# Modulation loads on ScalarE's queue, softmax statistics written in runs of four, norm roots by tile, and the output weights of the dilated layer rounded sooner

## The reference, cut to what matters

```python
for g, (window, dil) in enumerate(DIL_GROUPS):
    qkv = (h @ w_in[:, base:base + 3 * MIXER_WIDTH]).reshape(B, T, 3, DIL_HEADS, DIL_HEAD_DIM)
    o, lse = dilated_group(rope(q), rope(k), v, window, dil)
wts = jax.nn.softmax(jnp.stack(lses, axis=0), axis=0)
o = jnp.einsum('gbth,gbthd->bthd', wts, jnp.stack(outs, axis=0))
```

```python
shift, scale, gate = jnp.split((silu(c) @ w_mod + b_mod)[:, None, :], 3, axis=-1)   # w_mod: 1024 x 3072 per layer
h = rms(x, g_pre) * (1.0 + scale) + shift
```

## Time and profile before

| | |
|---|---|
| median of 3 runs | 1818.31 us (1816.36 to 1821.93) |
| the profiled execution | 1822.41 us, span 1820.6 us |
| mean granted clock of TensorE | 0.954 |
| busy: TensorE, VectorE, ScalarE, GpSimd | 93%, 52%, 35%, 11% of the span |
| DMA | 161 MB, 89 GB/s over the span |

### The profile page before, as it was taken

One profiled execution on the slowest core, in us unless ns is written; L12 is line 12 of the kernel. 1 busy time (PEld: TensorE's weight loads), 2 busy tenths in 40 slices (PEclk: granted clock), 3 DMA queues, 4 the chain that ended last, 5 costly groups with the idle time before them and its releaser, 6 DMA issues.

```text
span 1820.6 us, 22789 instructions
## 1 busy us (share of the span) xinstructions
PE 1684.1 (93%) x8922; PEld 1309.3 (72%) x8922; DVE 953.1 (52%) x1671; ACT 641.0 (35%) x1226; POOL 194.3 (11%) x221
## 2 busy tenths in 40 slices
PE   7999977989999989969999999979998999997997
PEld 6866756877788878847888878845556877785553
DVE  1233272265655555554446777446674377664462
ACT  3254342333223323343312434244442234423331
POOL 3045223100000000031001000000101010000000
PEclk9998988999999999989999999969999999997699
DMA  7211043322663673641322110230002332221000
GB/s 265 67 39 58 24 175 97 103 75 74 176 175 83 169 175 89 211 97 50 121 101 86 52 52 31 93 127 1 12 12 87 104 122 56 73 93 70 1 12 35
DMA packets 170834, 161.34 MB, mean 89 GB/s; under 512 B 39958, under 2 KB 153864, under 8 KB 170696
## 3 DMA queue, kind: packets, MB, share of 16 engines
q1 hardware_dynamic: 167592, 150.04, 27.4%
q0 software_dynamic: 2848, 9.74, 1.5%
q10 hardware_dynamic: 288, 0.10, 0.0%
HBM read 149.80 MB, written 11.18 MB: 88 GB/s over the span
## 4 chain that ended last, share of the span: by engine, by line
PE 76%; DVE 14%; ACT 4%; issue 4%; POOL 1%; DMA 1%; ACTq 0%; DVEq 0%; POOLq 0%
PE psum L2398 42%; PE psum L2369 11%; PE psum L2861 7%; PE psum L2427 6%; PE psum L2418 4%; DVE arena L1829 2%; PE psum L2532 2%; PE psum L2471 2%; PE psum L2452 1%; DVE stat L2278 1%; DVE wring_r L1906 1%; DVE arena L1808 1%; DVE psum L2227 1%; DVE wring_r L1912 1%; DVE arena L1805 1%
## 5 line engine op out<-in xcount | busy, mean ns | idle before, releaser
L2398 PE MATMUL psum<-hT_r,wring_r 128*128 128x512 f32 (+1 forms) x1768 | 595.9, 395 | 7.7 <-ACT arena L1441 3.0
L2398 PEld LDWEIGHTS psum<-hT_r,wring_r 128*128 128x128 f32 (+1 forms) x1768 | 331.8, 188 | 89.3 <-issue 13.2
L2398 PE MATMUL psum<-arena_r,wring_r 128*128 128x256 f32 (+2 forms) x1416 | 381.8, 336 | 2.6 <-DVE arena_r L1952 1.8
L1441 ACT ACTIVATE arena<-psum 128x512 f32<-128x512 f32 (+5 forms) x255 | 149.4, 611 | 475.9 <-PE psum L2398 259.6
L2398 PEld LDWEIGHTS psum<-arena_r,wring_r 128*128 128x128 f32 (+1 forms) x1416 | 228.2, 190 | 32.0 <-issue 4.2
L2369 PE MATMUL psum<-arena 128*128 128x96 f32 (+9 forms) x1460 | 238.0, 390 | 4.7 <-ACT arena L1441 2.4
L2369 PEld LDWEIGHTS psum<-arena 128*128 128x128 f32 (+5 forms) x1460 | 170.7, 203 | 68.8 <-issue 45.8
L2398 PE MATMUL psum<-arena_r 128*128 128x512 f32 (+2 forms) x680 | 210.1, 350 | 0.0
L2427 PE MATMUL psum<-ident,arena 128*128 128x128 f32 (+2 forms) x1028 | 142.1, 290 | 47.9 <-DVE arena L1808 18.4
L2427 PEld LDWEIGHTS psum<-ident,arena 128*128 128x128 f32 (+2 forms) x1028 | 122.4, 149 | 69.0 <-DVE arena L1808 20.3
L2398 PE MATMUL psum<-hT_r,arena_r 128*128 128x512 f32 (+1 forms) x408 | 163.2, 400 | 5.4 <-DVE wring_r L1906 3.7
(11 more groups left out here) (223 smaller groups left out, 1933.3 us busy)
## 6 DMA issues: line engine op xcount, KB each, us to landing
wring<-in_w_in_b SPq DMA_DIRECT2D x54, 512.0 KB, 5.9
arena<-in_w_mod SPq DMA_DIRECT2D x16, 1536.0 KB, 10.1
wring<-in_w_in SPq DMA_DIRECT2D x16, 1536.0 KB, 6.8
wring<-in_w_out SPq DMA_DIRECT2D x8, 2048.0 KB, 11.0
wring<-in_w_in_a SPq DMA_DIRECT2D x5, 1536.0 KB, 6.6
arena<-x_dram SPq DMA_DIRECT2D x3, 2048.0 KB, 11.4
wring<-in_w_in SPq DMA_DIRECT2D x6, 1024.0 KB, 5.5
arena<-ebias_dram SPq DMA_DIRECT2D x144, 32.0 KB, 1.8
```

Of the source, the lines that this page charges most:

```text
L1441: return nc.scalar.activation(out, in_, ACT.Copy, scale=scale)
L2398: ins_ = nc.tensor.matmul(b[0:hi.shape[2], 0:width], w[:, k], v[:, k], start=k + p == 0, stop=(k, p) == (KT - 1, 2))
```

## The change

- **Modulation loads.** They leave SP's list. ScalarE issues them: `mod_after` names the step after which each goes out (piece 0 after `mPV A`, 1 after `mPV B`, piece n + 1 after `mod` n), with a wait until TensorE has done that step. Piece 14 gets a buffer of its own and is loaded after `BS 4`, piece 15 after `mod` 13.
- **Modulation products.** The first moves to between `wout A` and `hT B`; one of head 4 goes; in head 5 two stand directly behind `BS 5` and none between the gates. They are 0 | 1, 2 | three in each of heads 1 to 3 | 12, 13 | 14, 15.
- **Statistics.** Group 0 is saved in two DMAs of 128 runs of four floats, in a DRAM layout of its own, and loaded back element by element in four DMAs of 32 partitions. So four saves and six loads, before three and three. In SP's order they now come directly behind `BS h`, and the bias transfers behind them.
- **Roots by tile.** GpSimd takes a tile's root ahead of its save; VectorE scales tile t - 1 after the additions of tile t; `hT B` turns the first three tiles for 7 of the 8 blocks as they come.
- **Output weights.** All four residues of each half on VectorE, in both layers; `wide B 1` moves from behind `BPV 5` to directly behind `wide B 0`, with other room.

```diff
--- before.py
+++ after.py
@@ -166,7 +166,21 @@
     add("", "outs", "wout", "A", 0, (6, 7))
+    chunk_no = itertools.count()
+
+    def modulation():
+
+        n = next(chunk_no)
+        if n:
+            l, j = divmod(n - 1, MODS)
+            add("v", "modC", l, j)
+            if j == MODS - 1:
+                add("", "modT", l)
+        if n < 2 * MODS:
+            add("v", "mod", *divmod(n, MODS))
+
     add("v" * 8, "wout", "A")
+    modulation()
     add("v" * 8, "hT", "B")
@@ -178,19 +192,6 @@
 
-    chunk_no = itertools.count()
-
-    def modulation():
...
     for h in range(BH):
@@ -201,14 +202,16 @@
             add("aav", "Bproj", h + 1, 1)
-            modulation()
+            if h + 2 < BH:
+                modulation()
             add("avav", "BT", h)
             add("aav", "Bproj", h + 1, 2)
         else:
+            modulation()
             add("", "wide", "wout", "B", 0)
+            add("", "wide", "wout", "B", 1)
             add("a", "gate", "B", 5)
             add("", "Bw", h)
-            modulation()
             add("a", "gate", "B", 6)
@@ -216,7 +219,6 @@
     add("", "outs", "wout", "B", 0, (5,))
-    add("", "wide", "wout", "B", 1)
     add("v" * 6, "wout", "B")
@@ -601,7 +603,7 @@
         xn = at(6144, TT, D)
-        mslot = at(10240, KT, MODC)
+        mslots = [at(10240, KT, MODC), at(14336, KT, MODC)]
         modpart = at(29184, MODC)
@@ -689,11 +691,11 @@
         wide_room = {("wout", "A"): [18688 + 1024 * i for i in range(8)],
-                     ("wout", "B"): [17408 + 1024 * i for i in range(6)] + [6144, 7168]}
+                     ("wout", "B"): [17408 + 1024 * i for i in range(6)] + [27136, 28160]}
 
         gate_dram = dram("gate_dram", [2, 2, D])
         x0_dram = dram("x0_dram", [T, D])
-        st0_dram = dram("st0_dram", [BH, 2, T])
+        st0_dram = dram("st0_dram", [BH, P // DIL, 2, DIL, TT])
         st12_dram = dram("st12_dram", [BH, 4, T])
@@ -876,7 +878,7 @@
             if n < split_bounds[2]:
-                return (24576, 28664, 27640)[u]
+                return (24576, 6144, 7168)[u]
             return 6144 + KT * P * u
@@ -1106,6 +1104,10 @@
 
+        mod_last = 2 * MODS - 1
+        mod_after = {("mPV", "A"): 0, ("mPV", "B"): 1, ("BS", BH - 2): mod_last - 1, mod_key(mod_last - 2): mod_last}
+        mod_after.update({mod_key(n): n + 1 for n in range(1, mod_last - 2)})
+
         block = ctx.enter_context(nc.Block())
@@ -1126,15 +1128,13 @@
             items.append((order_of[("gate", "B", 7)], "x0_back", None))
-            for n in range(2 * MODS):
-                items.append((order_of[mod_key(n - 1) if n else ("mPV", "B")], "mod", n))
             for h in range(BH):
-                items.append((order_of[mod_key(3 * h - 1) if h else ("BS", 0)] + 0.5, "stats", h))
+                items.append((order_of["BS", h] + 0.5, "stats", h))
             for l in range(2):
                 items.append((order_of[("nv", l)] + 0.5, "strips", l))
                 for kind in range(3):
                     n = 3 * l + kind
-                    items.append((order_of[("BS", n - 1) if n else ("Bproj", 0, 0)], "ebias", (l, kind)))
+                    items.append((order_of[("BS", n - 1) if n else ("Bproj", 0, 0)] + 0.7, "ebias", (l, kind)))
                 for kind in range(3):
@@ -1205,10 +1205,6 @@
                         late_vectors()
-                elif what == "mod":
-                    read_by_pe(sp, mod_key(arg - 1) if arg else ("mPV", "B"))
-                    _, l, j = mod_key(arg)
-                    sp.dma_start(mslot, cols_of(ins["w_mod_2"][l], j * MODC, MODC)).then_inc(mod_in, 16)
                 elif what == "ebias":
@@ -1246,14 +1242,18 @@
                     strided = lambda d: d.rearrange("c (i b) -> i c b", b=DIL)
-                    pairs = [(st0_dram[h], 0, natural, strided)]
-                    pairs += [(st12_dram[h, 2 * g - 2:2 * g], g, strided, natural) for g in (1, 2)]
-                    for d, g, save, _ in pairs:
-                        sp.dma_start(save(d), b_stat[:, b, g, 1] if g else stat_of(g, 0),
+                    drams = {g: st12_dram[h, 2 * g - 2:2 * g] for g in (1, 2)}
+                    for c in range(2):
+                        sp.dma_start(st0_dram[h, :, c], b_stat[:, b, 0, 0, c],
                                      allow_slow_non_contiguous=True).then_inc(st_saved, 16)
-                    sp.wait_ge(st_saved, 48 * (h + 1))
-                    for d, g, _, load in pairs:
-                        sp.dma_start(stat_of(g, 0) if g else b_stat[:, b, g, 1], load(d),
+                    for g, d in drams.items():
+                        sp.dma_start(strided(d), b_stat[:, b, g, 1],
+                                     allow_slow_non_contiguous=True).then_inc(st_saved, 16)
+                    sp.wait_ge(st_saved, 64 * (h + 1))
+                    for g, d in drams.items():
+                        sp.dma_start(stat_of(g, 0), natural(d), allow_slow_non_contiguous=True).then_inc(st_in, 16)
+                    for n in range(TT):
+                        sp.dma_start(stat_of(0, 1)[n * 32:n * 32 + 32], st0_dram[h, :, :, :, n].rearrange("r c q -> r (c q)"),
                                      allow_slow_non_contiguous=True).then_inc(st_in, 16)
@@ -1347,11 +1347,6 @@
                     nc.gpsimd.tensor_tensor(rest, w, hi.bitcast(F32), ALU.subtract).then_inc(av_rest0, 1)
-                elif kind == "wide":
-                    for q in (0, 2):
-                        _, w, hi, rest = wide_parts(*key[1:], q)
-                        pool.wait_ge(wide_hi, wide_hi_count(*key[1:], q))
-                        nc.gpsimd.tensor_tensor(rest, w, hi.bitcast(F32), ALU.subtract).then_inc(wide_lo_even, 1)
                 elif kind == "Ao":
@@ -1363,10 +1358,9 @@
                             evacuated(pool, key, 2 * t + 1)
+                            norm_roots("B", t)
                             pool.dma_start(x0_dram[t * P:(t + 1) * P], x[:, t]).then_inc(x0_saved, 16)
                         pool.dma_start(dil_rope, consts["dil_rope"]).then_inc(rope_in, 16)
-                        for t in range(TT):
-                            norm_roots("B", t)
                     else:
@@ -1784,6 +1778,13 @@
                     square("C1" if t < TT else "c1", t % TT)
+                if key in mod_after:
+                    n = mod_after[key]
+                    read_by_pe(act, key)
+                    if n == 0:
+                        read_by_pe(act, ("gate", "A", 7))
+                    act.dma_start(mslots[n == mod_last - 1], cols_of(ins["w_mod_2"][n // MODS], n % MODS * MODC, MODC)).then_inc(
+                        mod_late if n == mod_last - 1 else mod_in, 16)
 
@@ -1906,11 +1907,11 @@
                 elif kind == "wide":
-                    for q in (1, 3):
+                    for q in range(4):
                         _, w, hi, rest = wide_parts(*key[1:], q)
                         dve.wait_ge(wide_hi, wide_hi_count(*key[1:], q))
                         nc.vector.scalar_tensor_tensor(rest, w, 1.0, hi.bitcast(F32), ALU.mult,
-                                                       ALU.subtract).then_inc(wide_lo_odd, 1)
+                                                       ALU.subtract).then_inc(wide_lo, 1)
                 elif kind == "outs":
@@ -2066,9 +2067,10 @@
                             norm_scale("C0", t)
+                        elif t:
+                            norm_scale("B", t - 1)
                     if ph == "A":
-                        for t in range(TT):
-                            norm_scale("B", t)
+                        norm_scale("B", TT - 1)
                 elif kind == "Bproj":
@@ -2413,7 +2415,7 @@
                         pe.wait_ge(out_lo, out_count(name, l, st, k))
-                        pe.wait_ge(wide_lo_odd if q % 2 else wide_lo_even, wide_lo_count(name, l, n, q))
+                        pe.wait_ge(wide_lo, wide_hi_count(name, l, n, q))
                     for p, (v, w) in enumerate(((x_hi, rounded), (x_lo, rounded), (x_hi, rest[:, k]))):
@@ -2445,11 +2447,16 @@
                     pe.wait_ge(silu_c, 1)
-                    pe.wait_ge(mod_in, 16 * (l * MODS + j + 1))
+                    n = l * MODS + j
+                    if n == mod_last - 1:
+                        pe.wait_ge(mod_late, 16)
+                    else:
+                        pe.wait_ge(mod_in, 16 * (n + 1 - (n == mod_last)))
+                    w = mslots[n == mod_last - 1]
                     b = claim(pe, key, 0)
                     for k in range(KT):
                         g = GROUP * (k % GROUPS)
-                        ins_ = nc.tensor.matmul(b[g:g + GROUP, 0:MODC], siluc[:, k], mslot[:, k], start=k < GROUPS,
+                        ins_ = nc.tensor.matmul(b[g:g + GROUP, 0:MODC], siluc[:, k], w[:, k], start=k < GROUPS,
                                                 stop=k >= KT - GROUPS)
@@ -2503,6 +2510,16 @@
                     done(ins_)
```

(10 more changed lines are left out.)

16 lines of the change are left out of this document (3 added, 13 removed).

## The result

The changed kernel takes 1788.1 us (median of 4 runs, 1785.7 to 1792.3); the kernel before, on the same chip, 1819.7 us: a ratio of 0.983, 95% interval 0.981 to 0.986. It is 31.6 us faster in the medians. The profiled run spans 1786.2 us, where the kernel before spanned 1820.6. The changed kernel was run once more beside the last experiments: 1786.9 us (median of 6), ratio 0.982 (0.980 to 0.985).

A forecast was written before the change was run, and what follows sets the result against it. TensorE, busy 93% of the span, was taken as the bound, so gains must come from its idle time or lower-clock stretches. Five terms, 3.0 + 4.8 + 9.5 + 8.1 + 9.1 = 34.5 us, gave 1783.8 us; range 1775 to 1801.

The forecast's parts named there:

- Term 1: Start of `wout A`: residues on VectorE alone bring the product's seventh step sooner; 3.0 us gained, bounds 1 and 3.7.
- Term 2: Hand-over from `wout A` to `hT B`: earlier gate product 3.3 us, moved modulation product 1.5; sum 4.8, bounds 2 and 7.
- Rival C: Hand-over stays bound by x0 save and ScalarE's split, `wout A` by the clock: 3 instead of 7.8 us, 1788.6; chance 0.13.
- Term 3: Heads 0 to 4: waits for modulation loads, caused by SP's order, and the slower clock vanish; 9.5 us, bounds 6 and 9.5.
- Term 4: Last head: products ahead of gate 5 and faster statistics saves start `BT 5` earlier; 8.1 us, bounds 3.2 and 12.0.
- Rival A: Last head: statistics saves stay slow, a fixed price of small writes; its gain falls to 3.2 us, 1788.7; chance 0.18.
- Rival B: Heads: bias DMAs delay chunk loads, so ScalarE, VectorE and TensorE wait; 12 of 31 us reach TensorE: 1796; chance 0.13.
- Rival D: ScalarE held at issuing its loads, ahead of `Bproj` evacuations: slower than before, 1838 at 3.6 us per issue; chance 0.03.
- Term 5: `wout B`: the 6.11 us idle gap from late rounding and its slower clock vanish; 9.1 us, bounds 7 and 9.1.

The follow-up runs named there:

- experiment 3: Changed kernel with half of the residues of the output weights of layer A back on GpSimd: 1793.1 us, ratio 0.986 to the kernel before.
- Experiment 6: Changed kernel with x0 saved in halves of a tile, ahead of the root: 1784.7 us, ratio 0.978 to the kernel before.
- Experiment 9: Kernel before with only the modulation loads moved to ScalarE's queue: 1813.7 us, ratio 0.996 to the kernel before.
- experiment 10: Kernel before with only the new layout of the statistics (group 0 in runs of four): 1804.1 us, ratio 0.992 to the kernel before.
- experiment 2: Changed kernel with the statistics of group 0 written in single elements again: 1794.6 us, ratio 0.988 to the kernel before.
- experiment 1: Changed kernel with the modulation loads issued by SP again, bias DMAs still behind the statistics: 1862.6 us, ratio 1.025 to the kernel before.
- Experiment 4: Changed kernel with the second half of the dilated layer's output weights rounded late again: 1791.2 us, ratio 0.986 to the kernel before.
- experiment 5: Changed kernel with the context and final norm's weights loaded early, right after the last but one modulation product: 1781.4 us, ratio 0.976 to the kernel before.

## Why the prediction was right, and where it was not

The forecast was 1784 us, 34.5 us faster by five terms; measured are 31.6 us. The sum is closer than its terms: they gave 2.4, 2.3, 10.0, 11.7 and 5.2 us where 3.0, 4.8, 9.5, 8.1 and 9.1 were taken.

- **Term 1 (3.0).** Up to the first modulation product (before: to the end of `wout A`) 2.4 us, by the table and by experiment 3 alike (2.5). The seventh step started 3.95 us sooner when both traces are laid on the end of gate A 7 (5.39 less 1.44), and the low clock took part back, as weighed: its 174 matmuls take 41.3 us now, 39.7 before.
- **Term 2 (4.8), mis-sized: 2.3.** 1.4 for the moved product and 0.9 for the rest. The failed step is the landing of the last save: the text let the residues start at 312.1 and allowed 314.9 at worst; laid on the end of `wout A`, which came 3.8 us sooner, they started at 314.6. The save was issued 2 us later, behind the root, and met a DMA share of 0.98. It landed in 8.6 us, and so it did in the kernel before, where it was issued at 304.16; the 2.9 to 4.0 us of the earlier trace rows are the three saves ahead of it. The text took a place inside that range where only the last save counts. So the gate product starts 3.4 us sooner, not 6. The clock then took 2.5 (from the gate product to its silu 8.3 us, before 5.8), where I had reckoned 2.2. Rival C described this half rightly. Experiment 6 shows what the hand-over could give.
- **Term 3 (9.5): 10.0, its cause half right.** 7.9 of it are the waits, as taken, and 2.1 the lower clock, of which the text counted 1.6, behind the longest wait alone. I put the term down to the queue of the loads alone. Experiment 9 shows 4.8 us for the queue and experiment 10 shows 7.8 for the layout of the statistics; they don't add, as either removes the same four short waits. The step that failed is that the layout was priced in the last head alone. SP's wait for the saves stands ahead of the loads that SP issues afterwards, so a faster save pays in the other heads too. The longest of the waits, in head 3, came from bias issues and from a landing of 15.7 us, where the text reckoned with the median of 10.1.
- **Term 4 (8.1), mis-sized: 11.7.** The saves take 4.6 us instead of the 8.5 taken, so `BT 5` runs behind gate 7 with no wait at all, near the upper bound of 12.0. The 10.4 us that TensorE waited here did not come from SP's order: the load left at the end of product 14 (experiment 9), into the one buffer that both products shared.
- **Rival A** fails. The Trainium skill, page "DMA: Bandwidth & Descriptors", section "Specifications", has one limit, 512 B, below which a DMA reads, modifies and writes. No run here shows whether the chip does that; but the time is not one and the same below 512 B. With 4-byte elements the saves of a head take 11.3 to 15.8 us from issue to the next issue (experiment 2), with runs of 16 bytes, half the writes, 4.3 to 8.7. Fewer and longer writes pay far below that limit; which of the two it is, no run separates.
- **The rule on queues** of the Trainium skill (the same page, section "Issuing engines are not separate DMA queues") says that another issuing engine saves only sequencer time. The traces agree: with the queue alone changed (experiment 9) a load lands in 10.0 us in the median, before in 10.1. The Trainium skill calls the time that it takes to start a DMA usually small. What was gained here is not that time but the wait for what stood ahead of the loads in SP's order: 4.8 us of the 7.7 in experiment 9 (the rest came in head 5, with a landing of 11.5 us instead of 16.4), and 74 us in experiment 1.
- **Rival B** fails: ScalarE waits longer for chunks (9.7 us at most), and no wait of TensorE follows. **Rival D** fails: an issue holds ScalarE 0.4 to 0.6 us.
- **Term 5 (9.1), mis-sized: 5.2.** The step that failed is that no other bound of the stage was looked for. The gap went and the product ran at full clock, but what now sets the end of the stage is VectorE's chain of norms: four tiles of some 7.5 us each, through ScalarE's square and GpSimd's root and back twice. It starts when x0 and the context are back, 27.3 us behind the issue of x0's load, before 26.5. With GpSimd free of residues the context's load leaves 10 us sooner after that issue (6.7 instead of 16.7 us), now beside x0's 2 MB, and takes 16.2 us instead of 5.4. Experiment 4 shows that the gap is worth 1.8 us as things stand, experiment 5 that with the context out of the way the stage takes 54.0 us, 8.5 less than before: nearly the 9.1.
- **Not foreseen:** the unchanged work behind the first `nkc` product took 957.3 us instead of 958.7, which no experiment explains and which lies within the scatter of the traces (954.8 to 959.6).

That the forecast came within 3 us is luck: term 4 was 3.6 us too low, terms 2 and 5 together 6.4 too high. Terms 3 and 5 lie outside their own bounds (6 to 9.5, and 7 to 9.1), so the single terms deserved wider ones.

## What to carry to other kernels

A wait in the order of an issuing queue delays everything that the queue issues later (here 4.6 us in four waits, in heads where TensorE never waited for the statistics themselves). Price a slow transfer by what stands behind its wait, in every stage, and not only where its own data is due. Before a step is moved forward in such an order, look at what it is moved past: here one move without the other cost 74 us. And before light work is spread over a gap of TensorE, ask what runs directly ahead of the next product: here the product started 2.9 us sooner at the lower clock and ended 0.4 us sooner.

## What the runs showed of the hardware that was not expected

- The saves of statistics: from 1,536 short writes per head to 768, and nothing else changed (experiment 2), the time from issue to the next issue fell from 11.3 to 4.6 us in head 5, more than in proportion. With the layout alone changed (experiment 10, ten transfers a head instead of six) the landings of all statistics transfers went from 1.7/6.1/19.2 (least, median, most) to 1.9/2.6/12.5 us.
- Half a tile of x0 (256 KB) took 7.8 us to land, a whole tile (512 KB) 8.6, at a DMA share of 0.98 or more, where the others of 512 KB took 3.0.
- The loads of 1.5 MB landed in 7.1 to 16.4 us in the kernel before, and in 7.0 to 18.4 in experiment 9 (median 10.1 and 10.0). The two waits that were left in experiment 9 came from the landings of 18.4 and 11.5 us.
- The same kernel, traced twice: spans 1786.2 and 1778.8 us. Of the 7.4 us, 3.0 arise before gate A 7 ends, 2.0 in `wout A`; heads 0 to 4 agree to 0.01 us. A single span says little below 0.4%; a stage that is bound by TensorE at full clock can be compared to a hundredth of a microsecond.
